# A router on the raw residual, and modulation sums on VectorE, in a fused transformer block

## The chip, the cores and the metric

The kernel runs on one core of one Trainium2 chip. The metric is the device time of one execution in microseconds (us); the time of the kernel before is the median of three. The profile is of one further execution. Engines: TensorE (PE; its weight loads, PEld, are listed apart), VectorE (DVE), ScalarE (ACT), GpSimd (POOL) and the DMA queue that SyncE (SP) fills.

## What is computed

One block over 256 tokens of width 1024, all in fp32, cut to what matters here:

```python
mod = (silu(c) @ w_ada + b_ada)                       # 6 x 1024: modulation
shift1, scale1, gate1, shift2, scale2, gate2 = jnp.split(mod, 6, axis=-1)
h = rms_norm(x, norm1_g) * (1 + scale1) + shift1
... # gated convolution and 8 heads of latent attention on h, merged
x = x + gate1 * (merged @ w_o)
h2 = rms_norm(x, norm2_g) * (1 + scale2) + shift2
g_logits = h2 @ w_rg + b_rg                           # 4 groups: softmax, top 1
e_logits = h2 @ w_re + b_re                           # 8 experts each: top 2 of the group
out = sum over the two experts of weight * SwiGLU(h2) # 32 experts, inner width 256
x = x + gate2 * out
```

## The kernel before

The residual stands transposed in SBUF, `xT[128, 8, 256]`: partitions are channels within a tile k of 128, the free side is tokens. An fp32 matmul shows as two MATMUL and two LDWEIGHTS records.

**Modulation.** `w_ada` comes in 12 items of 512 columns. Items 0 to 3 are done at the start. Items 4 to 11 go one to each head of the attention stage, through one place in SBUF, `ada_beside`, which is the place of expert 3. For each, TensorE makes 32 matmuls (`ada_item`, 32 columns of weights from `c_rep`, four column groups of the array), ScalarE copies the sum to `ada_rows`, TensorE turns it, and VectorE adds the bias into `mod`.

**Heads.** For each of 8 heads h TensorE projects q and k, makes the five convolution and gate tiles of head h + 1 (`conv_tile`, 8 matmuls of 256 columns each), the scores (`s_ready`), and the attention. While VectorE and ScalarE make the softmax of head h (`max_ready`, `exp_done`, `p_ready`), TensorE makes the modulation item and the conv tiles 3 and 4. In the last head the early part of the output projection stands in the tiles' place. VectorE normalises q and k, merges head h - 1 (`merge`), makes the taps of the next convolution (`conv_taps`) and its gate (`conv_gated`). GpSimd makes two additions in each head (`sq_joined`), for which the norm's matmuls wait. In even heads the rotary part of q is made for two heads.

**Transfers.** All are asked for by SyncE in program order: a wait holds up all that stands behind it. A ring of two places in `wmix` holds the weights of head h and h + 1 (`mix_load`, waits for `v_ready`); the item's is `beside_load`, the experts' `expert_load`. Experts 0 to 2 come during heads 1 to 3, 3 to 6 around the output projection, and each later one when TensorE is done with the expert seven before it (`next_expert`).

**Router.** After the output projection VectorE adds to the residual, ScalarE squares it (`x2sq_ready`), TensorE sums the squares over channels with `ones`, ScalarE and VectorE make the reciprocal root (`r2`), VectorE scales `xT` into `hT`, ScalarE adds `shift2` (`h2_ready`). TensorE multiplies by the router (36 columns) and turns `hT` to rows by token, `h2_rows`; VectorE picks the top ones (`first_of_max`), TensorE counts ranks, VectorE makes slots (`slot_tok`) and a table of windows for each expert. Bands of PSUM for the experts' output are cleared by matmuls of `ones` with a zero `ycomb`.

**Experts.** Each window of 32 slots gathers its rows by a matmul with a one-hot `sel`, turns them (`turn_rows`), VectorE copies them to `xw`, and TensorE makes gate, up and down. The count of windows is read from the table at run time; with these inputs it is 35: 32 experts, three of which need two windows.

Of the kernel before, what the change touches and what calls it, by code (L numbers as in the profile page):

```python
# [36 lines left out]
                ("group_no", GROUPS), ("expert_no", PER_GROUP), ("inv_freq", 1), ("row_no", 1))  # L37
# [29 lines left out]
WORK = 7040  # L67


def block_kernel(nc, xT_d, pos_d, small_d, const_d, ada_d, lat_d, mix_even_d, mix_odd_d, wo_d, ex_d, out_d):  # L70
    with ExitStack() as ctx:
# [81 lines left out]
        wins = piece(3 * EXPERTS)  # L153
        lg = piece(72).rearrange("p (t n) -> p t n", t=TT)
        r2s, r2 = comb_both[:, 0:T], comb_both[:, T:2 * T]
        g_work = piece(5 * 8).rearrange("p (a t n) -> p a t n", a=5, t=TT)
        e_work = piece(6 * 16).rearrange("p (a t n) -> p a t n", a=6, t=TT)
        s_work = piece(24).rearrange("p (a t) -> p a t", a=12)
        oh = piece(4 * 64).rearrange("p (a t n) -> p a t n", a=4, t=TT)
        slots = piece(64).rearrange("p (t n) -> p t n", t=TT)  # L160
        slot_oh = piece(128).rearrange("p (c t n) -> p c t n", c=2, t=TT)
        slot_tok = piece(4).rearrange("p (c t) -> p c t", c=2)
        split_tail = piece(GU_COLS // 2 + DOWN_COLS)
# [15 lines left out]
        ada_rows = wex[:, OWN - 1, GU_COLS:GU_COLS + P]  # L179

# [35 lines left out]
        wo_ready, x2_ready, x2sq_ready, x2ss_ready, r2_ready, h2_ready = (sem("wo_ready"), sem("x2_ready"), sem("x2sq_ready"), sem("x2ss_ready"), sem("r2_ready"), sem("h2_ready"))  # L216
        h2_scaled = sem("h2_scaled")
        lg_ready, h2r_ready, h2r_copied = sem("lg_ready"), sem("h2r_ready"), sem("h2r_copied")
# [4 lines left out]
        ada_copied, ada_turned = sem("ada_copied"), sem("ada_turned")  # L223
        mod_ready = sem("mod_ready")
# [7 lines left out]

        MIX0 = 1
# [11 lines left out]
        def _(sp):  # L245
# [67 lines left out]
            sp.wait_ge(h2r_ready, 4)  # L313
# [46 lines left out]
        def _(act):  # L360
# [69 lines left out]

            for a in range(4):
                act.wait_ge(x2_ready, a + 1)
                nc.scalar.activation(hT[:, 2 * a:2 * a + 2, :], xT[:, 2 * a:2 * a + 2, :], ACT.Square).then_inc(x2sq_ready, 1)
            act.wait_ge(x2ss_ready, 1)
            nc.scalar.activation(r2s, ps[:, 3, 0:T], ACT.Sqrt, bias=eps_1[:], scale=1.0 / D).then_inc(r2_ready, 1)
            for k in range(KT):
                act.wait_ge(h2_scaled, k + 1)
                nc.scalar.activation(hT[:, k, :], hT[:, k, :], ACT.Identity, bias=mod[:, 24 + k:25 + k]).then_inc(h2_ready, 1)  # L438
            for b in range(4):
                act.wait_ge(h2r_ready, b + 1)  # L440
                nc.scalar.copy(h2_rows[:, b // 2, (b % 2) * 512:(b % 2) * 512 + 512], ps[:, 1 + b, :]).then_inc(h2r_copied, 1)
                if b == 1:
                    act.wait_ge(gdiff_ready, 1)
                    nc.scalar.activation(g_work[:, 1], g_work[:, 1], ACT.Exp).then_inc(gexp_ready, 1)
            act.wait_ge(ediff_ready, 1)
            nc.scalar.activation(s_work[:, 6, :], s_work[:, 5, :], ACT.Exp).then_inc(eexp_ready, 1)
# [16 lines left out]
        def _(pe):  # L463
# [91 lines left out]

            early = [(m, k) for m in range(8) for k in range(HEADS - 2)]
# [12 lines left out]
            for h in range(HEADS):  # L569
# [12 lines left out]
                if h % 2 == 0:  # L582
                    wqr = slot[:, WQR_AT:MIX_COLS[0]].rearrange("p (k c) -> p k c", k=3)
# [44 lines left out]
                pe.wait_ge(ada_landed[3], 16 * h + 32)  # L628
                ada_item(ada_beside, ps[:, 0, 0:P]).then_inc(ada_done, 1)
# [5 lines left out]
                nc.tensor.transpose(ps[:, 0, P:2 * P], ada_rows, ident).then_inc(ada_turned, 1)  # L635
                if h + 1 < HEADS:
# [27 lines left out]
            a0 = SMALL["w_router"][0]  # L664
            for t in range(TT):
                for k in range(KT):
                    last = mm(ps[:, 6, 64 * t:64 * t + 36], hT[:, k, t * P:(t + 1) * P], small[:, a0 + 36 * k:a0 + 36 * k + 36], k == 0, k == KT - 1)
            last.then_inc(lg_ready, 1)
            for b in range(4):
                for q in range(4):  # L670
                    last = nc.tensor.transpose(ps[:, 1 + b, q * P:(q + 1) * P], hT[:, (b % 2) * 4 + q, (b // 2) * P:(b // 2 + 1) * P], ident)
                last.then_inc(h2r_ready, 1)

            pe.wait_ge(y_cleared, 1)
            for b in (1, 3):
                mm(ps[:, 4 + b, :], ones[:], ycomb, True, True)
            pe.wait_ge(onehot_ready, 1)
# [466 lines left out]
```

## Time and profile before

| | us |
|---|---|
| median of 3 runs | 542.34 (541.79 to 544.69) |
| time of the profiled execution | 544.22 |
| its span | 542.4 |
| TensorE busy | 502.8 (93%) |
| VectorE busy | 186.9 (34%) |
| ScalarE busy | 150.5 (28%) |
| GpSimd busy | 153.2 (28%) |

The span is what the profiler sees from the first to the last instruction; the time of the same execution has 1.8 us around it. Busy shares are means over stages of different kind. Moved in all: 161.89 MB, a mean of 298 GB/s. The mean granted clock of TensorE is 0.975 of its full 2.4 GHz; it has two levels, and 0.50 in a window means 1.2 GHz throughout.

### The profile page before, as it was taken

What the parts mean: (1) busy time and instruction counts of PE and PEld (TensorE: products, weight loads), DVE (VectorE), ACT (ScalarE), POOL (GpSimd) and SP (SyncE); (2) the same over time, 40 slices, a digit from 0 to 9 for tenths busy, and PEclk for the clock granted to TensorE, in tenths of its full rate; (3) what the DMA queues carried; (4) which work ended last, traced back from release to release, by engine and by line L of the source; (5) the groups of instructions that cost most, each with busy time, mean ns of one, the idle gap of its engine ahead of it and who ended that gap; (6) DMA issues with size and microseconds to landing.
All of it is one profiled execution on the core that took longest, in us unless ns stands there. A gap on an engine that the chain in (4) does not pass through costs nothing.

```text
span 542.4 us, 14805 instructions
## 1 busy us (share of the span) xinstructions
PE 502.8 (93%) x6173; PEld 393.7 (73%) x6174; DVE 186.9 (34%) x567; ACT 150.5 (28%) x281; POOL 153.2 (28%) x195
## 2 busy tenths in 40 slices
PE   4799999999999999999999597999899899899994
PEld 3587888888888888888888475675566556566663
DVE  0631624233423342334213352333233332333333
ACT  3012222223222322232301432232233223223221
POOL 0000010101010101010100005676677667667662
PEclk9799999999999999999999778999999999999999
DMA  8996327394959473725329931979999999999982
GB/s 351 431 434 247 146 77 277 126 429 181 424 213 430 171 284 131 282 88 197 121 106 381 408 112 57 411 266 428 425 434 433 428 431 428 431 430 428 433 350 79
DMA packets 10689, 161.89 MB, mean 298 GB/s; under 512 B 1184, under 2 KB 2464, under 8 KB 3104
## 3 DMA queue, kind: packets, MB, share of 16 engines
q1 hardware_dynamic: 10656, 161.40, 72.5%
q8 instruction: 27, 0.44, 0.3%
q14 instruction: 6, 0.05, 0.0%
HBM read 160.35 MB, written 1.05 MB: 298 GB/s over the span
## 4 chain that ended last, share of the span: by engine, by line
PE 84%; DMA 9%; issue 2%; DVE 2%; ACT 1%; SPq 0%; DVEq 0%; ACTq 0%
PE ps L465 80%; DMA wex<-in_ex 6%; DMA wex<-in_ada 3%; PE ps L710 1%; PE ps L736 1%; ACT act L438 1%; PE ps L711 1%; DVE xT L1032 1%; DVE work L926 0%; PE ps L644 0%; PE ps L643 0%; PE ps L635 0%; PE ps L645 0%; DVE work L967 0%; SPq L279 0%
## 5 line engine op out<-in xcount | busy, mean ns | idle before, releaser
L465 PE MATMUL ps<-act,wmix 128*128 128x256 f32 x864 | 195.0, 382 | 1.0 <-DVE act L816 1.0
L465 PEld LDWEIGHTS ps<-act,wmix 128*128 128x128 f32 x864 | 162.3, 191 | 25.1 <-issue 3.7
L350 POOL TENSOR_SCALAR work<-trig,work 128x256 f32<-128x256 f32 x70 | 65.0, 938 | 71.8 <-issue 62.5
L465 PE MATMUL ps<-wex,work 128*32 128x128 f32 (+1 forms) x1840 | 70.3, 300 | 10.4 <-issue 9.0
L336 POOL TENSOR_TENSOR work<-work,trig 64x256 f32<-64x256 f32 x8 | 5.8, 720 | 252.2 <-ACT work L403 150.6
L465 PE MATMUL ps<-work 32*128 32x256 f32 (+6 forms) x864 | 72.8, 375 | 0.7 <-ACT work L459 0.5
L465 PEld LDWEIGHTS ps<-wex,work 128*32 128x32 f32 x1840 | 50.0, 111 | 28.1 <-issue 13.1
L465 PEld LDWEIGHTS ps<-work 32*128 32x128 f32 (+3 forms) x864 | 47.4, 168 | 13.7 <-issue 3.8
L456 ACT ACT_TABLE_LOAD x35 | 44.9, 1283 | 1.3 <-issue 0.7
L354 POOL TENSOR_TENSOR work<-work,trig 128x512 f32<-128x512 f32 x35 | 44.7, 1278 | 0.0
L465 PE MATMUL ps<-act,work 128*32 128x256 f32 (+1 forms) x704 | 42.2, 360 | 0.9 <-issue 0.9
L357 POOL TENSOR_TENSOR work<-work 128x256 f32<-128x256 f32 x35 | 25.5, 729 | 49.5 <-PE ps L465 49.5
L1017 DVE COPY work<-ps 128x128 f32<-128x128 f32 x35 | 10.2, 292 | 83.2 <-PE ps L465 83.2
L459 ACT COPY work<-ps 128x256 f32<-128x256 f32 x35 | 13.0, 373 | 80.7 <-PE ps L465 80.7
L465 PE MATMUL ps<-wmix,work 128*32 128x128 f32 (+2 forms) x704 | 32.8, 294 | 2.0 <-issue 2.0
L465 PEld LDWEIGHTS ps<-wmix,work 128*32 128x32 f32 (+1 forms) x704 | 25.3, 117 | 9.1 <-DVE work L1025 5.6
L465 PE MATMUL ps<-wex,c_rep 128*32 128x128 f32 x768 | 25.1, 286 | 3.3 <-DMA wex<-in_ada 3.3
L465 PEld LDWEIGHTS ps<-act,work 128*32 128x32 f32 x704 | 21.7, 110 | 8.8 <-DVE work L1025 2.8
L465 PEld LDWEIGHTS ps<-wex,c_rep 128*32 128x32 f32 x768 | 21.5, 115 | 7.2 <-issue 3.5
L1025 DVE COPY work<-ps 128x256 f32<-128x256 f32 x35 | 14.9, 425 | 33.9 <-PE ps L711 33.9
L456 ACT ACTIVATE work<-ps 128x64 f32<-128x64 f32 x35 | 7.8, 224 | 61.9 <-PE ps L736 61.9
L465 PE MATMUL ps<-work,wmix 128*128 128x256 f32 x104 | 23.8, 379 | 0.0
(177 smaller groups left out, 433.1 us busy)
## 6 DMA issues: line engine op xcount, KB each, us to landing
wex<-in_ex SPq DMA_DIRECT2D x20, 3072.0 KB, 18.4
wex<-in_ada SPq DMA_DIRECT2D x12, 2048.0 KB, 10.7
wmix<-in_ex SPq DMA_DIRECT2D x8, 3072.0 KB, 19.4
wmix<-in_mix_even SPq DMA_DIRECT2D x4, 3200.0 KB, 10.7
wmix<-in_mix_odd SPq DMA_DIRECT2D x4, 3008.0 KB, 10.7
work<-in_ex SPq DMA_DIRECT2D x4, 2048.0 KB, 19.5
wmix<-in_wo SPq DMA_DIRECT2D x2, 2048.0 KB, 7.3
act<-in_ex SPq DMA_DIRECT2D x4, 1024.0 KB, 14.9
```

The lines of the kernel that those rows point to most:

```text
L336: nc.gpsimd.tensor_tensor(k_sq[0:ROPE, :], k_sq[0:ROPE, :], k_rope_sq[0:ROPE, :], ALU.add).then_inc(sq_joined, 1)
L350: nc.gpsimd.tensor_scalar(comb_both[:, rows], slot_row[:, rows], lane_now, None, ALU.is_equal).then_inc(comb_half, 1)
L354: nc.gpsimd.tensor_tensor(comb_both, comb_both, weight_row, ALU.mult).then_inc(comb_pair, 1)
L357: nc.gpsimd.tensor_tensor(comb, comb_both[:, 0:T], comb_both[:, T:2 * T], ALU.add).then_inc(comb_ready, 1)
L438: nc.scalar.activation(hT[:, k, :], hT[:, k, :], ACT.Identity, bias=mod[:, 24 + k:25 + k]).then_inc(h2_ready, 1)
L456: nc.scalar.activation(silu_t, ps[:, 1, 0:2 * WIN], ACT.Silu).then_inc(silu_done, 1)
L459: nc.scalar.copy(y_sb, ps[:, 2, 0:T]).then_inc(y_copied, 1)
L465: return nc.tensor.matmul(out, lhsT, rhs, start=start, stop=stop, **kw)
L710: nc.tensor.transpose(ps[:, 0, P:2 * P], rows_sb[:, 0:P], ident)
L711: nc.tensor.transpose(ps[:, 0, 2 * P:3 * P], rows_sb[:, P:T], ident).then_inc(rows_turned, 1)
L1017: v.tensor_copy(gu_sb, ps[:, 0, 0:P]).then_inc(gu_copied, 1)
L1025: v.tensor_copy(xw_v, xw_ps).then_inc(xw_ready, 1)
```

## The change

**Modulation items 4 to 11.** VectorE sums them in eight steps, one for each tile k of the contraction (`ada_steps`), into `ada_sum[128, 512]`: steps 0 to 4 behind the gated convolution of the coming head, steps 5 to 7 within the head. TensorE sums over partitions only, four matmuls with `ones` instead of 32. The item's transfer waits for VectorE's last step (`ada_summed`) instead of TensorE's matmuls, and stands ahead of the ring's in SyncE's order.

```diff
             def beside_load(j):
-                sp.wait_ge(ada_done, 4 + j)
+                if j == 0:
+                    sp.wait_ge(ada_done, 4)
+                else:
+                    sp.wait_ge(ada_summed, j)
                 sp.dma_start(ada_beside, ada_d[4 + j]).then_inc(ada_landed[3], 16)
...
             for c in range(HEADS):
+                if c + 1 < HEADS:
+                    beside_load(c + 1)
                 if c + 2 < HEADS:
                     mix_load(c + 2)
...
                 if 1 <= c < OWN:
                     expert_load(c - 1, c - 1)
-                if c + 1 < HEADS:
-                    beside_load(c + 1)
...
-            sp.wait_ge(h2r_ready, 4)
+            sp.wait_ge(h2r_ready, 2)
+            sp.wait_ge(lg_ready, 1)
             split_load(last, 0)
...
-                pe.wait_ge(ada_landed[3], 16 * h + 32)
-                ada_item(ada_beside, ps[:, 0, 0:P]).then_inc(ada_done, 1)
+                pe.wait_ge(ada_summed, h + 1)
+                for q in range(4):
+                    last = mm(ps[q * WIN:(q + 1) * WIN, 0, 0:P], ones[:, 0:WIN], ada_sum[:, q * P:(q + 1) * P], True, True)
+                last.then_inc(ada_done, 1)
...
+            def ada_steps(j, steps):
+
+                w = ada_beside.rearrange("p (k c) -> p k c", k=KT)
+                if steps[0] == 0:
+                    dve.wait_ge(ada_landed[3], 16 * j + 32)
+                    dve.wait_ge(ada_done, 4 + j)
+                for k in steps:
+                    if k == 0:
+                        link(v.tensor_scalar(ada_sum, w[:, k, :], c_rep[:, k, 0:1], None, ALU.mult))
+                    elif k < KT - 1:
+                        link(v.scalar_tensor_tensor(ada_sum, w[:, k, :], c_rep[:, k, 0:1], ada_sum, ALU.mult, ALU.add))
+                    else:
+                        v.scalar_tensor_tensor(ada_sum, w[:, k, :], c_rep[:, k, 0:1], ada_sum, ALU.mult, ALU.add).then_inc(ada_summed, 1)
```

**Router.** `norm2_g * (1 + scale2)` is multiplied into the router's weights and into a stack of scaled identities, `turn_by`, by VectorE in head 7; `shift2` times the router is added to the bias in head 5. TensorE takes the unscaled residual as moving side, with 32 columns of router weights at a time, and the squares beside it: experts in column groups 0 and 1 of the array, groups in 2, squares in 3. VectorE copies the 128x256 result to `logits_t`, and two matmuls with the constant `fold` add the parts and turn them, 36 logits and the sum of squares for each token. The reciprocal root goes into rows as ScalarE's scale, and into the exponentials; logits are compared with the bias times the root instead. The selection is written with fewer operations. `shift2` is added in each window when `xw` is made.

```diff
+                if h == 5:
+                    for k in range(KT):
+                        last = mm(ps[:, 1, 0:36], mod[:, 24 + k:25 + k].broadcast_to([P, P]), small[:, a0 + 36 * k:a0 + 36 * k + 36], k == 0, k == KT - 1)
+                    last.then_inc(part_ready, 1)
...
-            for k in range(KT):
-                if k % 2 == 0:
-                    pe.wait_ge(x2sq_ready, k // 2 + 1)
-                last = mm(ps[:, 3, 0:T], ones[:], hT[:, k, :], k == 0, k == KT - 1)
-            last.then_inc(x2ss_ready, 1)
...
-            pe.wait_ge(h2_ready, KT)
...
+            for a in range(4):
+                pe.wait_ge(x2_ready, a + 1)
+                for i in range(2):
+                    k = 2 * a + i
+                    w = small[:, a0 + 36 * k:a0 + 36 * k + 36]
+                    mm(ps[i * WIN:(i + 1) * WIN, 5, 0:T], w[:, GROUPS:], xT[:, k, :], a == 0, a == 3, skip_group_check=True)
+                    mm(ps[2 * WIN:3 * WIN, 5, 0:T], w[:, 0:WIN], xT[:, k, :], k == 0, k == KT - 1, skip_group_check=True)
+                    if a > 0:
+                        squares_of(a - 1, i)
+            for i in range(2):
+                last = squares_of(3, i)
+            last.then_inc(lgt_ready, 1)
+            turn_x2(3)
+            pe.wait_ge(lgt_copied, 1)
             for t in range(TT):
-                for k in range(KT):
-                    last = mm(ps[:, 6, 64 * t:64 * t + 36], hT[:, k, t * P:(t + 1) * P], small[:, a0 + 36 * k:a0 + 36 * k + 36], k == 0, k == KT - 1)
+                last = mm(ps[:, 6, 64 * t:64 * t + 37], logits_t[:, t * P:(t + 1) * P], co("fold"), True, True)
             last.then_inc(lg_ready, 1)
...
+            turn_x2(13)
...
             gather(0)
+            spread(1, slot_tok)
             turn_rows(0)
```

What this moves in the instructions is seen in three places. The first is TensorE in an odd head, from the scores (`work 128x256`) to the softmax's transposes: before.

```order
L465 MATMUL ps<-work 128x256 x2
L465 MATMUL ps<-wex,c_rep 32x128 [waits ada_landed3]
L465 MATMUL ps<-wex,c_rep 32x128 x31
L465 MATMUL ps<-act,wmix 128x256 x8
L635 MATMUL ps<-const,wex 128x128 [waits ada_copied]
L465 MATMUL ps<-act,wmix 128x256 [waits mla_gate_ready]
```

And now:

```order
L481 MATMUL ps<-work 128x256 x2
L481 MATMUL ps<-wex,ones 32x128 [waits ada_summed]
L481 MATMUL ps<-wex,ones 32x128 x3
L481 MATMUL ps<-act,wmix 128x256 x8
L656 MATMUL ps<-const,wex 128x128 [waits ada_copied]
L481 MATMUL ps<-act,wmix 128x256 [waits mla_gate_ready]
```

`c_rep` is the conditioning vector, `wex` holds the item, `wmix` the conv tiles' weights. The 32 matmuls on the item are four on VectorE's sum, and the wait for the transfer is one for VectorE.

The second is TensorE from the last part of the output projection (`act,wmix`) to the first gather (`act,work 32x256`). Before, sums of squares (`act,ones`), router (`small,act`), transposes of `hT` (L671), and then the clearings (`work,ones 128x512`):

```order
L465 MATMUL ps<-act,ones 128x256 [waits x2sq_ready]
L465 MATMUL ps<-act,ones 128x256
L465 MATMUL ps<-small,act 128x36 [waits h2_ready]
L465 MATMUL ps<-small,act 128x36 x15
L671 MATMUL ps<-const,act 128x128 x16
L465 MATMUL ps<-work,ones 128x512 [waits y_cleared]
L465 MATMUL ps<-work,ones 128x512
L465 MATMUL ps<-work,const 128x32 [waits onehot_ready]
L465 MATMUL ps<-work,ones 128x32
L465 MATMUL ps<-work,const 128x32
L465 MATMUL ps<-work,ones 128x32 x2
L465 MATMUL ps<-const,work 128x128 [waits w_tok_ready,h2r_copied]
```

Now the router's matmuls on the residual (`xT,small`) with the squares, the turning (`act,xT`), the fold (`const,act 128x37`):

```order
L481 MATMUL ps<-xT,small 32x256 x2
L481 MATMUL ps<-work,ones 32x256
L481 MATMUL ps<-work,ones 32x256 [waits x2sq_ready]
L481 MATMUL ps<-work,ones 32x256
L481 MATMUL ps<-act,xT 128x128 x3
L481 MATMUL ps<-const,act 128x37 [waits lgt_copied]
L481 MATMUL ps<-const,act 128x37
L481 MATMUL ps<-act,xT 128x128 x13
L481 MATMUL ps<-work,ones 128x512 [waits y_cleared]
L481 MATMUL ps<-work,ones 128x512
L481 MATMUL ps<-work,ones 128x512 [waits h2r_copied]
L481 MATMUL ps<-work,ones 128x512 [waits lg_done]
```

All 16 router matmuls stand ahead of any wait for a scaled `hT`; the two clearings that stood behind the first spread now stand ahead of the rank (`work,const 128x64`), and wait for ScalarE's copies.

The third is SyncE's order of transfers in the heads. Before:

```order
L270 DMA wmix<-in_mix_odd 128x6016 [waits lat_ready]
L270 DMA wmix<-in_mix_even 128x6400 [waits v_ready]
L292 DMA wex<-in_ada 128x4096 [waits ada_done]
L270 DMA wmix<-in_mix_odd 128x6016 [waits v_ready]
L259 DMA wex<-in_ex 128x6144
L292 DMA wex<-in_ada 128x4096 [waits ada_done]
```

And now, where each item (`in_ada`) is ahead of its ring load (`in_mix`), and the expert's behind both:

```order
L278 DMA wmix<-in_mix_odd 128x6016 [waits lat_ready]
L303 DMA wex<-in_ada 128x4096 [waits ada_summed]
L278 DMA wmix<-in_mix_even 128x6400 [waits v_ready]
L303 DMA wex<-in_ada 128x4096 [waits ada_summed]
L278 DMA wmix<-in_mix_odd 128x6016 [waits v_ready]
L267 DMA wex<-in_ex 128x6144
```

## Rows read from the trace of the kernel before

**Rows 1.** Windows of three stages: us, busy time of each engine, TensorE's granted clock, DMA share, GB/s.
```profile
119.60:147.60 28.00, 28.00 (x194) 24.16 (x193) 10.02 (x26) 7.56 (x18) 1.40 (x2) 1.00 0.74 304
300.50:328.78 28.28, 18.96 (x102) 15.38 (x101) 14.48 (x61) 10.03 (x19) 1.85 (x2) 0.75 0.55 225
335.66:526.30 190.64, 179.43 (x3761) 119.66 (x3761) 61.40 (x226) 61.81 (x98) 132.32 (x164) 1.00 0.98 412
```

**Rows 2.** Timeline (start us, us, engine, line, operation, tile) at the end of head 2.
```profile
141.89 1.69 PEld L465 LDWEIGHTS ps<-wex,c_rep 128*32 128x32 f32 x64 [0.33 <-issue]
...
143.77 3.32 PEld L465 LDWEIGHTS ps<-act,wmix 128*128 128x128 f32 x16 [0.20 <-issue]
...
144.60 0.35 DVE L906 TENSOR_SCALAR work<-work 128x256 f32<-128x256 f32 x1
```

**Rows 3.** Timeline, VectorE in heads 2 and 3; in brackets its idle time before, and the releaser.
```profile
127.31 0.48 DVE L877 TENSOR_SCALAR work<-ps,small 128x256 f32<-128x256 f32 x1 [6.47 <-ACT work L403]
...
133.27 0.42 DVE L885 TENSOR_TENSOR work<-trig,ps 128x256 f32<-128x256 f32 x1 [3.84 <-PE ps L465]
...
160.78 1.75 DVE L888 RECIPROCAL work<-work 128x256 f32<-128x256 f32 x1 [4.65 <-ACT work L413]
```

**Rows 4.** Groups by line: a wide VectorE operation; busy us, mean ns.
```profile
L804 DVE TENSOR_TENSOR act<-xT,work 128x2048 f32<-128x2048 f32 x1 | 2.3, 2293 | 0.0
```

**Rows 5.** Timeline in head 3, GpSimd's second addition and VectorE's merge.
```profile
155.12 0.72 POOL L337 TENSOR_TENSOR work<-work 64x256 f32<-64x256 f32 x1
155.25 0.87 DVE L867 SCALAR_TENSOR_TENSOR act<-work,act 128x256 f32<-128x256 f32 x1
```

**Rows 6.** Timeline: the ring's transfer asked for, and its first use.
```profile
131.88 0.33 SPq L270 DMA_DIRECT2D wmix<-in_mix_even  x1
...
154.04 3.62 PE L465 MATMUL ps<-act,wmix 128*128 128x256 f32 x16
```

**Rows 7.** DMA issues of the page: count, KB each, median us from issue to landing.
```profile
wmix<-in_mix_even SPq DMA_DIRECT2D x4, 3200.0 KB, 10.7
```

**Rows 8.** Timeline from the last output projection to the first expert window.
```profile
296.81 3.43 PEld L465 LDWEIGHTS ps<-act,ones 128*128 128x128 f32 x16
...
306.91 6.90 PEld L465 LDWEIGHTS ps<-small,act 128*128 128x128 f32 x32 [6.67 <-ACT act L438]
...
314.00 0.23 DVE L933 TENSOR_TENSOR work<-ps,small 128x72 f32<-128x72 f32 x1 [7.70 <-PE ps L465]
...
316.35 1.28 ACT L444 ACT_TABLE_LOAD   x1
...
317.76 1.05 ACT L441 COPY act<-ps 128x512 f32<-128x512 f32 x2
...
319.57 0.23 DVE L970 TENSOR_TENSOR work<-work 128x64 f32<-128x64 f32 x1
...
320.96 0.97 PEld L465 LDWEIGHTS ps<-const,work 128*128 128x128 f32 x8
...
321.26 0.19 DVE L984 TENSOR_SCALAR work<-ps 128x32 f32<-128x32 f32 x1 [0.65 <-PE ps L465]
...
321.96 1.88 PE L465 MATMUL ps<-work,ones 128*128 128x512 f32 x4
...
323.76 0.23 DVE L999 TENSOR_TENSOR work<-work 128x64 f32<-128x64 f32 x1
...
324.67 1.07 PE L465 MATMUL ps<-act,work 128*32 128x256 f32 x16
...
328.78 3.25 PE L465 MATMUL ps<-wex,work 128*32 128x128 f32 x64 [1.98 <-issue]
```

**Rows 9.** Windows of 1 us: behind the idle stretch, and in the first expert window.
```profile
304.00:305.00 1.00, 0.00 (x0) 0.00 (x0) 1.00 (x3) 1.00 (x4) 0.00 (x0) 0.59 1.14 492
...
329.00:330.00 1.00, 1.00 (x24) 0.96 (x20) 0.00 (x0) 0.00 (x0) 1.00 (x2) 0.50 0.07 16
```

**Rows 10.** Waits: us in total, times, longest us.
```profile
PE ps L465 <- DMA wex<-in_ex: 1.0, 1, 1.0
```

More of the change, by code:

```diff
@@ new lines, in turn_x2, with squares_of @@
+            def turn_x2(count):
+                for k, t in turns[:count]:
+                    last = mm(ps[:, ROW_BANK[k // 4][t], (k % 4) * P:(k % 4 + 1) * P], xT[:, k, t * P:(t + 1) * P], turn_by[:, k, :], k % 4 == 0, True, skip_group_check=True)
+                    if k % 4 == 3 and t == TT - 1:
+                        last.then_inc(h2r_ready, 1)
+                del turns[:count]
+            def squares_of(a, i):
+                if i == 0:
+                    pe.wait_ge(x2sq_ready, a + 1)
+                return mm(ps[3 * WIN:4 * WIN, 5, 0:T], ones[:, 0:WIN], x2_sq[a][:, i, :], a == 0 and i == 0, a == 3 and i == 1, skip_group_check=True)
@@ L965, in _ @@
-            for c, e in ((0, 2), (1, 4)):
+            dve.wait_ge(lgt_ready, 1)
+            v.tensor_copy(logits_t, ps[:, 5, 0:T]).then_inc(lgt_copied, 1)
+            dve.wait_ge(rs_ready, 1)
+            dve.wait_ge(bias_ready, 1)
+            for t in range(TT):
+                last = v.scalar_tensor_tensor(lg[:, t, :], sm("b_router"), rs_tok[:, t:t + 1], ps[:, 6, 64 * t:64 * t + 36], ALU.mult, ALU.add)
+            last.then_inc(lg_done, 1)
+            v.reciprocal(r_tok, rs_tok).then_inc(r2_ready, 1)
@@ new lines, in _, with first_of_max @@
+            dve.wait_ge(lg_done, 1)
+            lg_g, lg_e = lg[:, :, 0:GROUPS], lg[:, :, GROUPS:]
+            top, first, d_top, e_top = s_work[:, 0, :], s_work[:, 1, :], s_work[:, 5, :], s_work[:, 6, :]
+            g_eq, g_no = g_work[:, 0], co("group_no")
+            masked, e_no = e_work[:, 0], co("expert_no")
+            e_eq = e_work[:, 1]
+            def first_of_max(values, top, eq, number, first):
+                link(v.tensor_reduce(top, values, AX_X, ALU.max))
+                for t in range(TT):
+                    last = v.scalar_tensor_tensor(eq[:, t, :], values[:, t, :], top[:, t:t + 1], number, ALU.is_equal, ALU.mult)
+                link(last)
+                link(v.tensor_reduce(first, eq, AX_X, ALU.min))
@@ new lines, in _ @@
+            first_of_max(lg_g, top, g_eq, g_no, first)
+            for t in range(TT):
+                last = v.tensor_scalar(g_work[:, 2, t, :], g_no, first[:, t:t + 1], LOW, ALU.not_equal, ALU.mult)
+            v.tensor_tensor(g_work[:, 1], lg_g, top.unsqueeze(2).broadcast_to([P, TT, GROUPS]), ALU.subtract).then_inc(gdiff_ready, 1)
+            link(last)
+            for t in range(TT):
+                last = v.tensor_tensor(masked[:, t, :].rearrange("p (g e) -> p g e", g=GROUPS), lg_e[:, t, :].rearrange("p (g e) -> p g e", g=GROUPS),
+                                       g_work[:, 2, t, :].unsqueeze(2).broadcast_to([P, GROUPS, PER_GROUP]), ALU.add)
@@ L966, in _ @@
+            link(last)
+            for c in range(2):
+                first_of_max(masked, s_work[:, 2 + c, :], e_eq, e_no, first)
                 for t in range(TT):
[L967 to L969 removed]
+                    last = v.tensor_scalar(oh[:, c, t, :], e_no, first[:, t:t + 1], None, ALU.is_equal)
+                link(last)
+                if c == 0:
+                    link(v.scalar_tensor_tensor(masked, oh[:, 0], LOW, masked, ALU.mult, ALU.add))
```

169 lines of the change are left out of this document (82 added, 87 removed).

## The prediction

> **What bounds the kernel now.** I read the windows by stage first. In an even head of the attention stage TensorE is busy for all of 28.00 us, at the full granted clock, while VectorE works 10.02 us and the DMA share is 0.74 [rows 1]. So whatever leaves TensorE's stream there is worth its whole length, as long as its new owner is on time. Next the stretch between the last output projection and the first expert window: 28.28 us in which TensorE is busy 18.96, at a mean granted clock of 0.75 [rows 1]. It is a chain that runs over all engines; the timeline shows it in order [rows 8]. Last the expert stage. From 335.66 to 526.30 the DMA share is 0.98 and TensorE is busy 179.43 of 190.64 us [rows 1]; yet TensorE waited for a weight transfer only once, 1.0 us [rows 10]. The 35 windows and the weight stream keep step: a load into a freed place is asked for when TensorE has finished an expert, and the windows end as the stream lets them. Both start from the first window, so the stage moves as a block with its start. The question is therefore how much earlier the first window's matmuls come than 328.78 [rows 8].
>
> **Heads: the modulation sums.** An item of the modulation is now 64 matmul records (two for each fp32 matmul). Their weight loads start at 141.89 and the next convolution tile at 143.77, 1.88 us later, 0.20 of them idle [rows 2]. Four matmuls, 8 records, stay; at the same pace (1.69 / 64 = 0.026 us each) they take 0.21, and I leave 0.2 for the gap. 1.88 - 0.41 is about 1.5 us a head, 12.0 us for eight. The bounds are 1.3 and 1.7 a head, from a remaining piece of 0.6 or of 0.2 us.
>
> VectorE takes over eight steps of 128x512 per item. A tensor_tensor of 2048 columns took 2293 ns, one of 256 took 0.42 us [rows 3, 4]: 1.04 ns a column. An operation with a per-partition scalar took 0.48 us at 256 columns [rows 3], so 0.48 + 0.27 = 0.75 us at 512, and an estimated 0.78 from one chained step to the next; the eight come to some 6.1 us. Added to 10 us busy this fits in a head; what counts is where. Steps 0 to 4 (3.8 us) follow the gated convolution. There VectorE sits idle for 6.47 us, up to 127.31; this cover shrinks by the 1.5 us that TensorE no longer needs, to 5.0. Steps 5 to 7 (2.3 us) stand in even heads ahead of the operation at 133.27, where it idles 3.84 us, and in odd heads ahead of the reciprocal at 160.78, idle 4.65 us [rows 3]. So they are hidden with 1.2 us or more to spare, and cost nothing on the path. If that cover were gone, each us late would be a us a head.
>
> The matmuls taken out also covered the softmax. VectorE has the probabilities ready at 144.95 (144.60 + 0.35, [rows 2]); TensorE's fourth convolution tile takes 3.3 us of weight loads from 143.77, from 142.3 in the new kernel, and a fifth follows. Nothing waits.
>
> In this trace a VectorE operation with two SBUF operands that meets GpSimd's addition (155.12 to 155.84) takes 0.87 us, twice the 0.42 of one of its width [rows 3, 5]. The new steps are of that kind, but stand before GpSimd's two additions and behind them. A collision would take 0.45 us of the 1.2 to spare: nothing in the sum. The Trainium skill (page "SBUF — State Buffer", section "SBUF: two separate sides") states that the two engines share a port pair under an exclusive lock, held for a whole instruction; by that rule a step that slides into the additions could lose both of them, and the second rival below has that in it.
>
> In head 5 eight matmuls of 36 columns are added (the shift's part of the router's bias). They load 128 columns of weights each and are paced by that: 6.90 us / 32 = 0.216 us a record at half clock [rows 8, 9], 0.108 at full, 16 records: 1.8 us on the path (bounds 1.7 and, at half clock, 3.5). The heads' sum is 12.0 - 1.8 = 10.2.
>
> **The queue.** In the trace the ring's transfer was asked for at 131.88, the item's only behind its matmuls (143.77) [rows 2, 6]. The item's now waits for VectorE's last step and stands ahead of the ring's. VectorE's last step would end near 131.8 (its idle time starts at 129.43, plus 2.3), just when the ring's own wait is met. The ring's then has the item's 2.1 MB ahead of it, 5.1 us at 412 GB/s [rows 1]; alone it took 10.7 us from issue to landing [rows 7]: it lands at 147.7. Its first use is at 154.04 [rows 6], 1.5 us earlier in the new kernel: 4.8 us to spare. With an expert's transfer a head moves 8.4 MB, 20.4 us, less than a head. No cost.
>
> **Between projection and experts.** All in the clock of the old trace; the heads' gain comes on top [rows 8].
> - Projections end at 296.8. Before: eight 256-column matmuls over the squares, then root, reciprocal, eight scalings and eight additions of the shift; the router's matmuls could only start at 306.91. Now: 16 router matmuls with 32 columns of weights and 8 over the squares share four column groups. In the gather 16 such records take 1.07 us, where 16 full ones take 3.43: they run side by side. The fullest group has 16 records at 0.214, 3.4 us, and two squares behind, 0.85. End 301.1.
> - Copy of the logits 0.42 with a handoff: 301.6; three turning matmuls end at 301.85; two matmuls with `fold` (4 records at 0.12, as the spread's 8 in 0.97) end near 302.5. Root of two columns and handoffs an estimated 0.3, two bias operations 0.35: logits at 303.2, where the old ones were at 314.23. 11.0 us.
> - The selection: from 314.00 to 319.57 26 VectorE operations at 0.21 us. Now 23, of which 8 don't wait for the one ahead (estimated at 0.08): 3.8 us. One-hots at 307.1.
> - TensorE is not there: 13 turning matmuls until 305.6, two clearings (1.88 / 2 = 0.94 each), then it waits for ScalarE's four scaled copies (the last three from 305.6 at 1.05 / 2: 307.3), two clearings more: 309.1. Rank: 6 records, 309.8. So 2 us of the one-hots' gain are lost here.
> - ScalarE: behind the copies the table load 1.28 and four small exponentials, 309.3; VectorE's weights end at 309.95, two small copies at 310.1. It enters the window count at 310.1 instead of 321.26.
> - Count to selection: 321.26 to 323.99 (323.76 + 0.23) is 2.73; two operations fewer at 0.21 make it 2.3: 312.4. The gather no longer stands behind the slots' spread, it starts at once instead of 0.7 later (324.67); but the spread (0.97) and ScalarE's copy of it (0.6 with handoff) follow, and TensorE's branch waits for that copy: 315.4. Then the table's values: TensorE's idle time ahead of the first window is 1.98 and called issue; with the turning matmuls ahead 2.3. First window at 317.7.
>
> 328.78 - 317.7 = 11.0. Its bounds: 8.5, if ScalarE's and TensorE's waits each cost 1 us more than here and the sweep 0.5; 12.5, if the clearings overlap the waits fully.
>
> **Small things.** In each window a PSUM copy becomes a PSUM addition of the same width. The addition of 256 columns with a PSUM operand takes 0.42 us [rows 3], about as the copy, so nothing. The constants grow by 93 columns, 48 KB: 0.1 us at the start, where transfers are waited for.
>
> **Sum.** 12.0 - 1.8 + 11.0 - 0.1 = 21.1 us. The profiled execution has a span of 542.4 and a time of 544.22, 1.88 above the median of 542.34. 542.34 - 21.1 = 521.2; the span would be 521.3.
>
> **Rivals.**
> 1. *Both gains arrive and the experts move as a block*: 521.2, own range 517.5 to 525 (heads 8.6 to 11.8, transition 8.5 to 12.5, 1 us of scatter). Chance 0.74.
> 2. *VectorE becomes late in the heads.* For it: only 1.2 us to spare in the tightest place, steps of a width that no row shows. At 1.1 us a step, steps 0 to 4 take 5.5 and cost 0.5 a head, and a collision with GpSimd 0.7 more: 1.2 x 7 = 8 us, 529. Against: the slope per column is well shown. Chance 0.08.
> 3. *TensorE's clock sinks again.* Behind its idle stretch it was at 0.59 in 304 to 305 and stayed low through the router's and the turning matmuls; it was at 0.50 again in the first window (329 to 330) [rows 9]. In the new kernel no gap ahead of 311 is above 0.5 us, but 1.4 and 3.0 us idle follow. If it falls in the first, gather, spread and first window cost 2 us more, 523. If it falls already in the sweep, TensorE's part of 301 to 311 doubles: 6 us, 527. Chance 0.08. The Trainium skill (page "TensorE: Matmul & The Clock Gate", Part 1) says that "activity releases the throttle"; in this trace records ran back to back for 6.9 us from 306.91 without that.
> 4. *The column groups don't run side by side*, so the router's move does not do what it says: 24 matmuls of 0.427 take 10.2 instead of 4.25, 527. Against: the gather's 1.07. Chance 0.04.
> 5. *The weight stream does not follow*: transfers of experts 3 to 6 (12.6 MB, 31 us) still fill the queue when the first place is freed, or the stream runs slower; part of the transition's gain is given back, 525 to 531. Against: they are asked for from head 7 on, over 40 us ahead. Chance 0.03.
> 6. *The other side: the ring starves.* The item's transfer is ahead, and all behind it waits for VectorE's sum. If this comes over 4.8 us behind the ring's own wait, each further us is lost in seven heads. At 4.8 + 21.1 / 7 = 7.8 us late the gain is gone; slower beyond. No row speaks for it: the sum is due at the same moment. Chance 0.03.
>
> Within 0.5% (2.7 us, about what a measurement of this kernel can tell from no change) lie only parts of 5 and 6. Faster 0.96, same 0.015, slower 0.025. The range for 8 in 10 takes in the first case and the clock's: 517.5 to 527.
>
> **What would show it.** Right: heads 1.5 us shorter with TensorE busy throughout; 8 records between scores and the fourth tile; VectorE's wide steps near 0.75 us; item transfers asked for beside the ring's; logits near 293, first window near 307.5; the distance from it to the end unchanged at 213.6. Wrong: waits of TensorE for the sums or the ring, a half clock ahead of the selection, or a longer expert stage.

## The result, and the profile after

The changed kernel takes 572.48 us (median of four, 571.34 to 577.07) where the kernel before takes 543.52 (also a median of four, 541.79 to 545.32): a ratio of 1.054, interval 1.048 to 1.060. It is slower by 29 us, where 21 us faster was predicted. The profiled execution took 571.72 us. From its page: span, TensorE's busy row, its granted clock in 40 slices, the queue that brings instructions, and the chain that ended last.

```profile
span 569.9 us, 14038 instructions
...
PE 498.4 (87%) x5757; PEld 383.8 (67%) x5758; DVE 228.3 (40%) x623; ACT 148.1 (26%) x276; POOL 152.9 (27%) x195
...
PEclk9799999999999999999998999879986999799999
...
q8 instruction: 51, 0.84, 0.6%
...
PE 85%; issue 9%; DMA 3%; DVE 1%; ACT 1%; SPq 0%; DVEq 0%; ACTq 0%
```

The two rows of the page of the kernel before that answer to the last two:

```profile
q8 instruction: 27, 0.44, 0.3%
...
PE 84%; DMA 9%; issue 2%; DVE 2%; ACT 1%; SPq 0%; DVEq 0%; ACTq 0%
```

TensorE's busy time fell by 4.4 us and the span grew by 27.5, so idle time was added. The chain has 9% "issue", time in which the engine waits for nothing that the profile names, instead of 2%. And the instruction queue moved 51 packets of 16 KB instead of 27.

**The heads went as predicted.** TensorE at the end of head 2 (start us, us, engine, line, operation, tile), answering to [rows 2]:

```profile
137.26 2.05 PE L481 MATMUL ps<-work 128*128 128x128 f32 x8
139.25 0.42 PE L481 MATMUL ps<-wex,ones 128*32 128x128 f32 x8
139.60 3.72 PE L481 MATMUL ps<-act,wmix 128*128 128x256 f32 x16
```

The sums over partitions start at 139.25 and the next tile at 139.60: 0.35 us instead of 1.88, so 1.5 saved. VectorE in the same head, the group of its wide steps on the page, and the queue, answering to [rows 3, 6]:

```profile
126.90 1.54 DVE L920 SCALAR_TENSOR_TENSOR wex<-wex,c_rep 128x512 f32<-128x512 f32 x2
...
130.56 0.42 DVE L942 TENSOR_TENSOR work<-trig,ps 128x256 f32<-128x256 f32 x1 [1.33 <-PE ps L481]
```

```profile
L920 DVE SCALAR_TENSOR_TENSOR wex<-wex,c_rep 128x512 f32<-128x512 f32 x48 | 36.0, 751 | 1.6
```

```profile
129.25 0.33 SPq L303 DMA_DIRECT2D wex<-in_ada  x1
129.62 0.43 SPq L278 DMA_DIRECT2D wmix<-in_mix_even  x1
```

The wide steps take 751 ns each. Behind those of this head (126.90) VectorE is still idle for 1.33 us, where the prediction had 1.2 or more to spare. The item's transfer is asked for right ahead of the ring's, and in no head does TensorE wait for the sums or for the ring.

**So did the way to the experts.** VectorE (the logits at L999, the window count at L1048), then TensorE (the router's bias in head 5, the gather, the first window), answering to [rows 8]:

```profile
292.77 0.41 DVE L999 SCALAR_TENSOR_TENSOR work<-small,work,ps 128x36 f32<-128x36 f32 x2 [1.11 <-ACT work L449]
...
300.32 0.20 DVE L1048 TENSOR_SCALAR work<-ps 128x32 f32<-128x32 f32 x1
```

```profile
219.21 1.87 PE L481 MATMUL ps<-small,mod 128*128 128x36 f32 x16
...
302.64 1.07 PE L481 MATMUL ps<-act,work 128*32 128x256 f32 x16 [1.29 <-DVE work L1061]
...
307.64 3.47 PE L481 MATMUL ps<-wex,work 128*32 128x128 f32 x64 [2.62 <-issue]
```

Logits at 292.8 to 293.2, the 36-column matmuls in head 5 took 1.87 us, and the first window's matmuls start at 307.64; the prediction had 293, 1.8 and 307.5. Up to here the changed kernel is 21.1 us ahead. That it agrees with the sum to the tenth is partly luck: in profiles of later kernels whose code ahead of the first window is the same but for some one-column matmuls, this window starts between 305.83 and 309.17.

**The experts lost it, and more.** From the first window to the start of the last additions to the residual, and two rounds of the loop over the seven places for experts' weights in between (windows: us, busy time of each engine, granted clock, DMA share, GB/s). After:

```profile
368.14:420.19 52.05, 42.61 (x805) 28.20 (x805) 13.33 (x49) 11.50 (x19) 25.12 (x32) 0.92 0.89 374
427.61:477.51 49.90, 43.17 (x805) 28.21 (x805) 13.33 (x49) 11.50 (x19) 25.13 (x32) 0.90 0.86 359
307.64:563.81 256.17, 207.83 (x4041) 138.33 (x4041) 66.84 (x245) 64.50 (x104) 140.58 (x175) 0.93 0.74 310
```

Before:

```profile
382.97:423.08 40.11, 38.65 (x805) 25.60 (x805) 13.33 (x49) 11.85 (x20) 26.91 (x35) 1.00 1.00 430
...
328.78:536.33 207.55, 195.52 (x4041) 130.19 (x4041) 66.78 (x245) 64.51 (x104) 139.79 (x173) 0.99 0.90 380
```

256.17 us instead of 207.55: 48.6 more, with the same 4041 matmul records. TensorE is busy 12.3 us longer for them, at a granted clock of 0.93 instead of 0.99, and idle 36.3 us longer. The low clock lies behind the standstills: it is 0.59 from 368.14 to 378.00 and 1.00 from there to the end of that round. Where it is idle stands in the timeline, in brackets. After, and below it before:

```profile
368.14 1.48 PE L481 MATMUL ps<-wex,work 128*32 128x128 f32 x19 [7.11 <-issue]
372.48 2.56 PE L481 MATMUL ps<-wex,work 128*32 128x128 f32 x43 [2.85 <-issue]
...
401.56 0.53 PE L481 MATMUL ps<-wmix,work 128*32 128x128 f32 x12 [2.17 <-issue]
...
427.61 1.48 PE L481 MATMUL ps<-wex,work 128*32 128x128 f32 x19 [7.43 <-issue]
...
484.73 1.48 PE L481 MATMUL ps<-wex,work 128*32 128x128 f32 x19 [7.22 <-issue]
```

```profile
382.97 1.95 PE L465 MATMUL ps<-wex,work 128*32 128x128 f32 x64 [1.45 <-issue]
...
424.45 1.96 PE L465 MATMUL ps<-wex,work 128*32 128x128 f32 x64 [1.37 <-issue]
```

368.14, 427.61 and 484.73 are the starts of the loop's second, third and fourth round. Going back to the loop's head costs 7.1 to 7.4 us there instead of 1.4, and more standstills follow at fixed places, the first behind 19 matmul records of the round. Others (401.56) lie further on in it. The waits of TensorE from 300 to 560 us name VectorE's selection twice, 1.3 and 0.3 us, both ahead of the first window, and never the weights (us in total, times, longest; before, "issue" had 12.0 us, 30 times, 2.0 at most, between 300 and 540):

```profile
PE ps L481 <- issue: 50.0, 43, 7.4
PE ps L481 <- DVE work L1061: 1.3, 1, 1.3
PE ps L481 <- DVE work L1041: 0.3, 1, 0.3
```

The transfers of one round (second round; GB/s in 40 slices, then packets and MB of a queue). After:

```profile
GB/s 457 435 419 342 88 0 0 0 264 347 424 446 397 446 435 408 463 413 413 463 424 397 463 413 446 413 424 446 430 380 474 430 413 446 430 408 430 408 369 419
...
q8 instruction: 9, 0.15, 0.9%
```

Before:

```profile
GB/s 403 403 498 403 356 379 490 450 395 474 442 450 450 427 427 411 427 450 450 427 403 450 403 427 450 474 427 379 450 403 427 427 521 403 403 427 427 427 427 450
...
q1 hardware_dynamic: 962, 17.84, 100.4%
q14 instruction: 1, 0.01, 0.0%
```

In the second round of the kernel before the instruction queue q8 brings nothing (it has no row), and the weights flow at 430 GB/s. In the changed kernel nine blocks of 16 KB come in the same round, and the weight stream falls to nothing for over 4 us, since TensorE stood still and freed no place in time (from 361 to 385 us SyncE waits for TensorE twice, 16.4 and 5.7 us): the weights wait for TensorE, not the other way round.

### The profile page after: what moved, and what is told of

The parts are those of the page before. It is cut to its first block, busy times and chain, and to the rows that moved or that the text cites. A ratio compares the mean times of both kernels' runs of the same rounds, so it can differ in the third digit from the quotient of the medians.

```text
span 569.9 us, 14038 instructions
## 1 busy us (share of the span) xinstructions
PE 498.4 (87%) x5757; PEld 383.8 (67%) x5758; DVE 228.3 (40%) x623; ACT 148.1 (26%) x276; POOL 152.9 (27%) x195
## 4 chain that ended last, share of the span: by engine, by line
PE 85%; issue 9%; DMA 3%; DVE 1%; ACT 1%; SPq 0%; DVEq 0%; ACTq 0%
PE ps L481 81%; DMA wex<-in_ada 3%; PE ps L777 2%; PE ps L751 2%; PE ps L752 1%; DVE xT L1094 0%; ACT act L454 0%; ACT L457 0%; PE ps L669 0%; PE ps L670 0%; PE ps L656 0%; PE ps L671 0%; SPq L287 0%; ACT work L457 0%; SPq L284 0%
## 5 line engine op out<-in xcount | busy, mean ns | idle before, releaser
L481 PE MATMUL ps<-wex,work 128*32 128x128 f32 (+1 forms) x1840 | 78.1, 316 | 37.0 <-issue 36.8
L481 PEld LDWEIGHTS ps<-wex,work 128*32 128x32 f32 x1840 | 54.7, 117 | 57.1 <-issue 41.3
L481 PE MATMUL ps<-act,work 128*32 128x256 f32 (+1 forms) x704 | 46.4, 376 | 4.8 <-issue 3.5
L481 PE MATMUL ps<-wmix,work 128*32 128x128 f32 (+2 forms) x704 | 34.2, 295 | 9.7 <-issue 9.7
L920 DVE SCALAR_TENSOR_TENSOR wex<-wex,c_rep 128x512 f32<-128x512 f32 x48 | 36.0, 751 | 1.6
L481 PEld LDWEIGHTS ps<-act,work 128*32 128x32 f32 x704 | 26.2, 115 | 12.9 <-issue 3.4
L1087 DVE TENSOR_TENSOR work<-ps,mod 128x256 f32<-128x256 f32 x35 | 14.9, 425 | 34.3 <-PE ps L752 34.3
```

What stands on the lines that cost most here:

```text
L481: return nc.tensor.matmul(out, lhsT, rhs, start=start, stop=stop, **kw)
L920: link(v.scalar_tensor_tensor(ada_sum, w[:, k, :], c_rep[:, k, 0:1], ada_sum, ALU.mult, ALU.add))
L1087: v.tensor_tensor(xw_v, xw_ps, shift2, ALU.add).then_inc(xw_ready, 1)
```

## The experiments

**The theory (T1).** TensorE's program is brought in blocks; 51 packets for 0.84 MB are 16 KB each. A matmul of fp32 is four instructions (two MATMUL, two LDWEIGHTS). A window has 230 records of both kinds together, and the loop over seven places, with its control instructions, 1,706 instructions by my count: 6.7 blocks, if a block holds 256. So it spans seven or eight blocks, depending on where in a block it begins. The change takes 834 instructions from ahead of it (416 records of each kind, and two), 66 more than three whole blocks, so the loop begins 66 instructions earlier in its block. The standstill behind 19 matmuls, 38 instructions and an estimated 13 of control, puts a block's border 51 instructions behind the loop's start in the changed kernel: it begins 205 into a block and spans eight. In the kernel before it began 15 into a block and spanned seven. T1: a loop of seven blocks stays where it is, one of eight is brought again in each round, when TensorE jumps back to the loop's head (the back edge).

The Trainium skill (page "Runtime: NRT & Kernel Launch", section "Instruction fetch mechanics") states 16 KiB blocks of 256 instructions and, for TensorE, room for 2048 of them; this case's packets have that size. It also states that a taken branch out of a two-page window forces a fetch. The second round of the kernel before goes back over seven blocks with no packet at all, so here the measurement decides against that sentence. By the room of 2048 a loop of eight blocks would stay too; in the runs below only loops over seven do.

The rivals were R1, the addition of `shift2` in each window; R2, the order of the weight stream; R3, TensorE's clock; R4, another engine's work behind a window.

**Shifting the code, nothing else** (four kernels). One-column matmuls ("pads") are put where TensorE waits 7.6 us at the start:

```diff
             pe.wait_ge(setup_done, 4)
+            for k in range(17):
+                mm(ps[0:1, 7, 0:1], ones[:, 0:1], ones[:, 0:1], True, True)
             for k in range(KT):
```

> The changed kernel with 17 one-column matmuls (four instructions each, 68 in all) put in front of TensorE's first work, where TensorE stands idle for some 7 us after the start; nothing else is different. Theory T1 (place of the code): the expert loop of 1,706 TensorE instructions now spans eight blocks of 256 instructions and is loaded anew in each round; 68 instructions further on it spans seven again. Then the stage from the first expert window to the end falls from 256 to about 213.6 us, the 7.1 to 7.4 us standstills at the loop's back edge go, and the time is about 521 to 524 us. The rivals (R1, the addition in the windows; R2, the weight stream; R3, the clock; R4, another engine's work behind the window) don't know of the place of the code: about 571 us.

> The changed kernel with 64 one-column matmuls in the same place, 256 instructions, one whole block. T1: the loop starts at the same place within a block as in the changed kernel, so the standstills stay: about 571 us (and the pads' own time lies in idle time). If instead any extra work at the start helped (a warmer clock, a later start of something), it would be as fast as with 17. R1 to R4: about 571 us.

> The kernel before the change with 48 one-column matmuls (192 instructions) in the same place. T1: its loop, which fits into seven blocks, is shifted to about the place that the changed kernel's has, spans eight, and the expert stage takes some 40 us more: about 583 us. R1 to R4: 542 to 544 us.

The fourth takes R1's suspect out: `v.tensor_copy(xw_v, xw_ps)` for the addition. It leaves `shift2` out of the experts' input, so it doesn't compute the whole block.

> The changed kernel with a plain copy in place of the addition of shift2 in each expert window (shift2 is left out of the experts' input, so part of the computation is missing). R1 (the addition is what each window waits for): 43 us over 34 windows or more, so back towards 521 to 530 us. T1 and R2 to R4: no change, about 571 us.

Measured, against 543.32 before (here and below, a median of four where an interval is given, else one execution): 17 matmuls 524.87 us (ratio 0.966, interval 0.963 to 0.969). 64 matmuls 576.81. The kernel before with 48 matmuls 592.26 (1.090, 1.083 to 1.098). The copy 572.92. The chip shows T1 from both sides: 68 instructions that compute nothing take 48 us off the changed kernel, 256 don't, and 192 add 49 us to the kernel before. R1 has fallen with the copy. R2 to R4 have no reason to depend on the number of pads in this way. With 64 the first standstill inside a round comes behind 19 records as without any, so this case too has the period in 256 instructions:

```profile
371.87 1.48 PE L481 MATMUL ps<-wex,work 128*32 128x128 f32 x19 [8.61 <-issue]
```

The page's rows for 17 matmuls, and for the kernel before with 48:

```profile
q8 instruction: 24, 0.39, 0.3%
...
PE 84%; DMA 10%; issue 2%; DVE 1%; ACT 1%; SPq 0%; DVEq 0%; ACTq 0%
```

```profile
q8 instruction: 55, 0.90, 0.6%
...
PE 84%; issue 9%; DMA 3%; DVE 2%; ACT 1%; SPq 0%; DVEq 0%; ACTq 0%
```

24 blocks instead of the changed kernel's 51, and 55 instead of 27 in the kernel before. 51 is 27 more than 24: nine in each of the three rounds that follow a back edge, as its trace has them.

**Each part alone, and the pads elsewhere.** VectorE's steps and the place of the item's transfer go with TensorE's matmuls; only the latter are shown.

```diff
--- modulation alone: the kernel before, with
+                pe.wait_ge(ada_summed, h + 1)
+                for q in range(4):
+                    last = mm(... ones[:, 0:WIN], ada_sum[:, q * P:(q + 1) * P], True, True)
...
--- router alone: the changed kernel, with
+                pe.wait_ge(ada_landed[3], 16 * h + 32)
+                ada_item(ada_beside, ps[:, 0, 0:P]).then_inc(ada_done, 1)
...
--- pads in the hole: the changed kernel, with
             spread(2, s_work[:, 8:10, :])
+            for k in range(15):
+                mm(ps[0:1, 0, 0:1], ones[:, 0:1], ones[:, 0:1], True, True)
```

> The modulation's part alone, on the kernel before: VectorE sums the heads' slices, TensorE has four matmuls for each instead of 32, the transfer asked for ahead of the ring's; router, residual and windows as before. It takes 8 x 112 TensorE instructions from ahead of the expert loop, which under T1 moves the loop's start by 128 instructions within a block and makes it span eight blocks. T1: heads 12 us shorter, expert stage about 42 us longer: about 572 us, slower than before. Without T1, the prediction's own sum for this part: 530.4 us.

> The same, modulation's part alone, with 36 one-column matmuls (144 instructions) at the start, where TensorE waits. T1: the loop spans seven blocks again; the heads' 12 us are left, less about 0.9 us that such pads cost at the start: 530.5 to 532 us. If the expert stage's loss came from the modulation's part itself (its transfers or VectorE), it is about 572 us with or without pads.

> The router's part alone: the changed kernel with the heads' modulation slices made by TensorE's 32 matmuls as before, their transfer asked for in the old place. This puts 8 x 112 TensorE instructions back ahead of the loop: under T1 its start lies some 77 instructions into a block, still within seven blocks by some ten instructions. T1: transition 11 us shorter, head 5 1.8 us longer, expert stage as before: about 533 us. If the router's part causes the long expert stage (R1, the addition, or its place in time), about 575 us or more; that would be so too if my count of the phase is ten instructions too low, which the standstills at the back edge would tell.

> The changed kernel with 15 one-column matmuls (60 instructions) not at the start but just before the first gather, where TensorE waits 1.3 us for VectorE. T1: as good as 17 pads at the start, since only the number of instructions ahead of the loop counts, and without the 0.9 us that pads at the start cost: 523.5 to 524.5 us. Were the pads' work at the start what helped, this would stay at 571 us.

Measured, against 543.31: modulation alone 562.34; with 36 pads 532.54 (0.980, 0.978 to 0.982); router alone 534.49 (0.984, 0.982 to 0.985); pads in the hole 522.47 (0.961, 0.958 to 0.964). Modulation alone was slow as expected, though by 10 us less. Its back edges tell why (second, third and fourth round of its loop):

```profile
375.18 3.19 PE L470 MATMUL ps<-wex,work 128*32 128x128 f32 x51 [7.38 <-issue]
...
424.79 3.31 PE L470 MATMUL ps<-wex,work 128*32 128x128 f32 x64 [1.45 <-issue]
...
473.72 3.19 PE L470 MATMUL ps<-wex,work 128*32 128x128 f32 x51 [7.50 <-issue]
```

Only two of three stand still for 7 us. T1 as stated has one at each, and it doesn't say why the middle one is missing; the instruction queue fits the pattern, 42 packets here, 18 more than 24. The standstill inside the first window's matmuls comes behind 51 records instead of 19: 64 instructions later, for a loop that begins 62 earlier. This is the block's border, seen from two kernels.

The kernel with the pads in the hole is the fastest of all. Its stage of the experts, its instruction queue, and its one wait for weights there:

```profile
305.83:514.33 208.50, 195.62 (x4041) 130.04 (x4041) 66.77 (x246) 64.46 (x104) 140.75 (x175) 0.99 0.89 378
```

```profile
q8 instruction: 24, 0.39, 0.3%
...
PE ps L481 <- DMA wex<-in_ex: 1.8, 1, 1.8
```

208.50 us and a clock of 0.99 again.

**The borders.** Same diff as the first, with other counts.

> The changed kernel with 11 one-column matmuls at the start (44 instructions). From the place of the standstill inside the first window of a round (after 19 matmuls in the changed kernel, 51 in the modulation's part alone, whose loop lies 62 to 64 instructions earlier in its block) I put the start of the changed kernel's loop 51 instructions ahead of a block's end. T1 with blocks of 256 instructions: with 44 the loop still begins in the old block and spans eight: slow, 560 to 575 us. A theory in which any shift helps: about 524 us.

> The same with 13 (52 instructions): one instruction past the block's end by my count (off by up to three), so the loop spans seven blocks: 524 to 525 us. It stands two matmuls from the run with 11, so if the one is slow and this one fast, nothing but the border of a block lies between them.

> The same with 37 (148 instructions): the loop starts 97 instructions into a block, and its end lies some ten into an eighth block. T1 as stated (eight blocks do not stay): slow, at least one standstill at the back edge of 7 us and some 550 to 575 us. If the border for staying is softer than a count of eight (the router alone, 77 into the block, was fast): 525 us.

> The same with 50 (200 instructions): the loop lies as it did in the modulation's part alone, which lost 30 us and stood still at the back edge only in every second round. If the loss depends on the place in the block and on nothing else of the change, this kernel shows the same pattern, standstills of 7.4 us in two of the four back edges, and 554 to 556 us.

Measured: 571.67, 525.38, 525.19 and 548.73 us. Two matmuls, eight instructions, are worth 46 us. The second round's start with 11 and, below, with 13:

```profile
374.08 3.62 PE L481 MATMUL ps<-wex,work 128*32 128x128 f32 x64 [12.65 <-issue]
...
430.45 3.64 PE L481 MATMUL ps<-wex,work 128*32 128x128 f32 x64 [12.41 <-issue]
```

```profile
363.25 1.96 PE L481 MATMUL ps<-wex,work 128*32 128x128 f32 x64 [1.49 <-issue]
```

The same with 50, to be held against modulation alone:

```profile
368.74 2.78 PE L481 MATMUL ps<-wex,work 128*32 128x128 f32 x47 [7.79 <-issue]
...
414.67 1.95 PE L481 MATMUL ps<-wex,work 128*32 128x128 f32 x64 [1.45 <-issue]
...
462.45 2.78 PE L481 MATMUL ps<-wex,work 128*32 128x128 f32 x47 [7.61 <-issue]
```

It shows that kernel's pattern, so the smaller loss belongs to where the loop lies in its blocks and not to the modulation's part (548.73 is 5 us under what I gave). With 37 I was wrong: eight blocks by my count, and fast.

**Start or length?** All these shift the loop as a whole. Two kernels keep its start (15 pads in the hole) and lengthen its body, and one stands between 37 and 50:

```diff
+                for k in range(more):        # 32 or 18, in the first of the loop's seven places
+                    mm(ps[0:1, 2, 0:1], ones[:, 0:1], ones[:, 0:1], True, True)
                 pe.wait_ge(act_done, n + 1)
```

> The changed kernel with 15 one-column matmuls ahead of the first gather (fast, 522.5 us, loop 9 instructions into a block) and 32 more inside the loop, in the first of its seven places (128 instructions, run four or five times, 64 records of some 0.029 us each: 1.9 us a time at most, 8 us in all). The loop starts where it starts in the fast kernel, but its end lies as far into an eighth block as in the modulation's part alone and in the kernel with 50. If the number of blocks that the loop spans decides: standstills of over 7 us at the back edge, about 25 us on top of the pads' own, 550 to 558 us. If the place of the loop's start in its block decides (a start in the later part being bad): only the pads' own time, 523 to 531 us.

> The same with 18 inside the loop (72 instructions): by my count the loop then ends five instructions ahead of the seventh block's end. Both theories: only the pads' own time, 522.5 to 527 us. It is the measure of what such pads cost by themselves.

> The changed kernel with 43 one-column matmuls at the start (172 instructions): the loop starts 121 instructions into a block, its end 35 into an eighth. With 37 (97 in, 11 over) it was fast, with 50 (149 in, 63 over) slow at two of three back edges. If seven blocks are the limit and my count of the loop's length is some ten too high, this is slow: 545 to 550 us. If the limit itself is soft, it is fast: 525 us.

Measured: 549.59, 527.46 and 552.80 us. With 18 in the loop 5.0 us were added, and no back edge stands still for over 1.5 us. 3.4 of them lie behind the first window's start (218.0 us from there to the end instead of 214.6), about the pads' own time; the other 1.8 lie ahead of it, where the two kernels are the same, and are scatter. 14 more in the loop add 22.1, and two of three back edges stand still again (those into the second and the fourth round):

```profile
368.63 3.64 PE L481 MATMUL ps<-wex,work 128*32 128x128 f32 x64 [8.02 <-issue]
...
464.85 3.64 PE L481 MATMUL ps<-wex,work 128*32 128x128 f32 x64 [7.45 <-issue]
```

So it is the number of blocks that the loop spans, not where it starts. And 43 pads are slow where 37 are fast: with the start known to some instructions, the loop that matters is between 1,672 and 1,695 long (1792 less 121, and less 97), my count of 1,706 was 11 to 34 too high, and seven blocks are the most that a loop without long standstills spans, in all fifteen runs and both kernels. The 552.80 with 43 have 42 packets and two long back edges of three (8.8 and 8.0 us).

## Why the prediction was wrong

- **The failed step** is in the first part: "Both start from the first window, so the stage moves as a block with its start", and its check, the distance from the first window to the end "unchanged at 213.6". It is 262.3 (569.9 - 307.64). With the loop in seven blocks it is 214.6 (520.4 - 305.83, pads in the hole) and 214.5 (523.5 - 309.04, 17 pads). I took the stage to be ruled by windows and weights alone, and costed the removed instructions by their time, not by what their number does to the place of the code behind them. "A longer expert stage" stood among the signs of an error, but none of the six rivals had this cause, and the chance of 0.025 for slower was too small for that.
- **The mechanism's price:** 48.6 us in the stage. 12.3 are matmuls that take longer, at a lower clock (0.93) behind the standstills; 36.3 are idle time. One round pays 18.0: its matmuls 3.96 (42.61 - 38.65), the back edge at its end 6.06 (7.43 - 1.37), the other standstills 7.98, the rest of the 11.94 by which 52.05 exceeds 40.11.
- **Heads, 12.0 less 1.8:** right. The modulation's part alone brings its first window to 317.06 from 328.78, 11.7 us, and the bias matmuls took 1.87 us. As times, 10.8 us (543.31 - 532.54), with 0.9 spent on pads at the start (first window at 318.00 with them, 317.06 without).
- **Transition, 11.0:** right. Router alone has its first window at 320.12, 8.7 us earlier; 11.0 - 1.8 = 9.2 was the term. Two steps on the way don't add up. Four clearings at 0.94 from 305.6 end at 309.4, not 309.1, which ScalarE's path hides either way; and gather, spread and copy from 312.4 end at 315.0, where 315.4 is given, 0.4 us with no term of its own. As times 8.8 us (543.31 - 534.49).
- **Sum, 21.1:** 20.8 measured (543.31 - 522.47) once the loop lies well. The four runs of that kernel spread from 520.6 to 523.9, so some of this agreement is luck.
- **Rivals:** VectorE late, column groups in series, starving ring: no trace of any; the wide steps' mean of 751 ns gives no sign of collisions with GpSimd. (The 0.42 us beside which the prediction holds 0.87 is that of an operation with a PSUM operand, not of one with two in SBUF.) The clock did sink, but in the experts and as a consequence. Of the weight stream there is a little: with the pads in the hole TensorE waits for weights 1.8 us (before 1.0, [rows 10]), and the stage is 1 us longer than before.
- **Open:** why a loop that reaches only some tens of instructions into its eighth block stands still at two back edges of three, and one that reaches further at all three. The first are those that begin 121 to 149 into a block, and the one that begins at 9 with 32 pads inside; the others begin at 205 or later. Why nine blocks come in a round of a loop over eight is open too. The back edge costs 12.0 to 12.7 us with 11 pads and 7 us without any; by my count the first border then lies 7 instructions behind the loop's start, ahead of its first matmul, so that two standstills may have become one, but 7.1 + 2.9 is only 10.0. No run here shows what is kept and what is dropped.

## What to carry to other kernels

Where TensorE's program has a loop of some thousand instructions, count them, and find where in a block of 256 the loop begins: an edit that only removes work ahead of it can move it across one more block's border. The signs are long "issue" waits at the loop's head and at fixed places of each round, and instruction packets that keep coming in its later rounds. Before an edit is judged, time it once more with a few one-column matmuls ahead of the loop, in a hole; here that turned 5.4% slower into 3.9% faster.

## What the runs showed of the hardware

- A loop over seven blocks of 256 instructions ran its second and third round without any instruction transfer (kernel before: back edge 1.4 us). One over eight was brought again: 7.1 to 12.7 us at two or all of three back edges, and up to 3.1 us at other places of a round (3.13 us in the trace of the kernel with the copy).
- The border is sharp: 525.38 us with 13 pads and 571.67 with 11.
- The loss falls also on the matmuls: in the changed kernel's third round TensorE needed 43.17 us for what takes 38.65, at a granted clock of 0.90 after the standstills.
